# Fourteen matmuls on a cleared tile at the start, and the first norm's sums and spread half a unit later

## What is computed

```python
def hybrid_layer(h, pos, states, p):
    u = rms_norm(h, p['norm_mix']) @ p['w_in']
    ...                                  # four head groups on the columns of u
    h = h + concat([y_ssd, y_ret, y_gla, y_lru]) @ p['w_out']
    hn = rms_norm(h, p['norm_ffn'])
    return h + (silu(hn @ p['w_gate']) * (hn @ p['w_up'])) @ p['w_down']

def rms_norm(x, w):
    return x * rsqrt(mean(x * x) + EPS) * w
```

## Time and profile before

| | |
|---|---|
| median of 3 timed runs | 1326.43 us |
| range | 1326.39 to 1328.45 us |
| the profiled execution's own time | 1321.0 us |
| its span, first to last instruction | 1319.2 us |
| outside the span (1321.0 - 1319.2) | 1.8 us |
| PE busy | 1294.3 us, 98% of the span |
| DVE busy | 856.5 us, 65% |
| ACT busy | 706.6 us, 54% |
| POOL busy | 293.3 us, 22% |

### The profile page before, as it was taken

How to read it: one execution, slowest core, us unless ns; L and a number is a source line. 1 busy time by engine, 2 the same in 40 slices (tenths; PEclk the granted TensorE clock), 3 DMA queues, 4 the chain that set the end, 5 groups by cost and what they waited for, 6 DMA issues and landing times.

```text
span 1319.2 us, 26928 instructions
## 1 busy us (share of the span) xinstructions
PE 1294.3 (98%) x10781; PEld 1244.7 (94%) x10781; DVE 856.5 (65%) x1697; ACT 706.6 (54%) x1209; POOL 293.3 (22%) x248
## 2 busy tenths in 40 slices
PE   7999999999999999999999999999999999999996
PEld 7988898999999999999999888899999999999996
DVE  6745766478853885378757557655888358835864
ACT  7626355576642674266564264556766246624641
POOL 1101001112242224324411010001123412351250
PEclk9999989999999999999999999999999999999998
DMA  8855745557744774476567475447477347735741
GB/s 266 220 115 139 178 107 115 119 132 168 168 131 107 171 168 129 105 171 172 140 149 161 112 169 145 97 115 166 104 178 193 100 105 173 191 106 105 170 126 68
DMA packets 63387, 189.73 MB, mean 144 GB/s; under 512 B 7584, under 2 KB 8864, under 8 KB 63264
## 3 DMA queue, kind: packets, MB, share of 16 engines
q0 software_dynamic: 27936, 67.12, 30.9%
q1 hardware_dynamic: 30672, 111.95, 26.8%
q10 hardware_dynamic: 4656, 8.95, 2.3%
HBM read 180.33 MB, written 5.43 MB: 141 GB/s over the span
## 4 chain that ended last, share of the span: by engine, by line
PE 88%; DVE 5%; ACT 2%; DVEq 2%; DMA 1%; issue 1%; ACTq 0%
PE bank L1638 47%; PE bank L1667 32%; PE bank L1581 1%; DMA raw<-weights 1%; PE bank L1834 1%; DVE up L1511 1%; DMA wl<-weights 1%; PE bank L1955 0%; PE bank L1961 0%; PE bank L1599 0%; ACT wl L540 0%; PE bank L1593 0%; DVE h L1572 0%; DVE ct L989 0%; DVE lru_x L989 0%
## 5 line engine op out<-in xcount | busy, mean ns | idle before, releaser
L512 POOL DMA_DIRECT2D wl<-weights x194 | 168.2, 867 | 882.4 <-ACT wl L540 871.8
L1638 PE MATMUL bank<-xh,wh 128*128 128x272 f32 x800 | 242.9, 304 | 8.1 <-DVE xl L938 7.8
L541 ACT ACTIVATE wh<-raw 128x512 fp32r<-128x512 f32 (+1 forms) x243 | 197.8, 815 | 89.4 <-PE bank L1638 79.3
L1638 PE MATMUL bank<-xh,wl 128*128 128x272 f32 x800 | 234.1, 293 | 0.0
L1638 PE MATMUL bank<-xl,wh 128*128 128x272 f32 x800 | 233.6, 292 | 0.0
L540 ACT ACTIVATE wl<-raw 128x512 fp32r<-128x512 f32 (+1 forms) x192 | 145.8, 760 | 121.5 <-PE bank L1638 109.4
L1667 PE MATMUL bank<-xh,wl 128*128 128x272 f32 x704 | 203.1, 289 | 0.0
L1667 PE MATMUL bank<-xh,wh 128*128 128x272 f32 x704 | 202.8, 288 | 0.1
L1667 PE MATMUL bank<-xl,wh 128*128 128x272 f32 x704 | 202.8, 288 | 0.0
L1638 PEld LDWEIGHTS bank<-xh,wh 128*128 128x128 f32 x800 | 153.9, 192 | 19.4 <-issue 17.4
L541 ACT ACTIVATE wh<-wsum 128x512 fp32r<-128x512 f32 x176 | 105.2, 622 | 123.5 <-DVE wsum L1408 83.2
(11 more groups left out here) (404 smaller groups left out, 3015.1 us busy)
## 6 DMA issues: line engine op xcount, KB each, us to landing
raw<-weights SPq DMA_DIRECT2D x202, 512.0 KB, 6.1
wl<-weights POOLq DMA_DIRECT2D x132, 256.0 KB, 5.6
wl<-weights POOLq DMA_DIRECT2D x62, 512.0 KB, 7.4
h<-x SPq DMA_DIRECT2D x4, 544.0 KB, 6.1
y<-h SPq DMA_DIRECT2D x4, 544.0 KB, 2.7
rv<-rk ACTq DMA_DIRECT2D x8, 136.0 KB, 2.5
tz<-rq ACTq DMA_DIRECT2D x8, 136.0 KB, 5.4
S<-s_ssd ACTq DMA_DIRECT2D x2, 512.0 KB, 7.3
```

The costliest lines, as they stand in the source:

```text
L512: nc.gpsimd.dma_start(wl[:, place(j)], weights[n][:, lo:lo + width], accum_op=ALU.add).then_inc(lo_added[BLOCK0[j] % RING], 16)
L541: a(wh[:, place(j)], whole, ACT.Copy).then_inc(hi_done, 1)
L1638: ins = mm(bank_, wt[:, at:at + P], xx[:, cols], start=(i == 0 and pass_ == 0), stop=(i == len(ks) - 1 and pass_ == 2))
```

## The change

Four edits:

- `IDLE_MATMULS = 14` matmuls of 128x128 by 128x512 stand ahead of everything on TensorE. Their input is the last block of the `wl` ring, their output the bank M[1]. Nothing reads the result, and the next use of M[1] overwrites it.
- VectorE clears that block as its first instruction (a MEMSET of 128x512), and TensorE waits for it (`cleared`).
- The sums of the first norm move from after step 2 to after step 3, and the spread from after step 3 to after step 4.
- ScalarE's `hi_first(2)` moves from behind the eighth square to behind the fifth.

```diff
+IDLE_MATMULS = 14
...
+        x_rounded, exact_done, cleared = sem("x_rounded"), sem("exact_done"), sem("cleared")
+        idle_tile = wl[:, (RING - 1) * BLOCK:RING * BLOCK]
...
                 a(sq[:, m % 2, :] if m else sq_sum[:], h[:, m, :], ACT.Square).then_inc(h_squared.sem, 1)
-            hi_first(2)
+                if m == KT // 2:
+                    hi_first(2)
...
+            v.memset(idle_tile.bitcast(F32), 0.0).then_inc(cleared, 1)
             v.memset(sp_x[:], 0.0).then_inc(dense_free.sem, 3)
...
+            pe.wait_ge(cleared, 1)
+            for _ in range(IDLE_MATMULS):
+                mm(M[1][:], idle_tile[:, 0:P], idle_tile, start=True, stop=True)
+
...
-                    if (s, layer) == (2, 0):
+                    if (s, layer) == (3, 0):
                         square_sums(layer, -1)
                         last_squares(layer, -1)
-                    if (s, layer) == (3, 0):
+                    if (s, layer) == (4, 0):
                         pe.wait_ge(exact_done, 1)
                         spread_rstd(layer, -1)
```

More of the change, by code:

```diff
@@ L415, in trunk @@
             signal(n, 1) for n in ("cent_mm", "cent_first", "cent_second", "cent_out"))
-        x_rounded, exact_done = sem("x_rounded"), sem("exact_done")
+        x_rounded, exact_done, cleared = sem("x_rounded"), sem("exact_done"), sem("cleared")
+        idle_tile = wl[:, (RING - 1) * BLOCK:RING * BLOCK]
         y_final, y_stored = sem("y_final"), sem("y_stored")
```

## The result

The changed kernel took 1329.59 us (median of 16 runs, 1326.05 to 1331.5), the kernel before 1326.39 us in the same comparison (16 runs, 1319.05 to 1328.45). The ratio is 1.0030, 95% interval 1.0021 to 1.0039: slower, by more than the 0.2% that separates a change from none. In a later comparison the ratio was 1.0047 (1.0031 to 1.0064). Four executions in the experiments took 1788 to 4785 us; the ratios leave them out, the medians given include them and would be up to 0.6 us lower without.

The account below looks back on a forecast made before the run. Until 44 us the spread's time, through VectorE's and ScalarE's chain, was taken as the bound. Sums at 20.4 by TensorE, plus 1.0 for the lock, gave 21.4 against 19.63: +1.8 us on 1326.43, 1328.2 us; range 1326.4 to 1330.2.

Parts of the forecast that it names:

- The 14 matmuls raise the clock, and TensorE reaches unit 0 at 2.4 GHz: TensorE's start: 14 matmuls take 6.0 us, from 1.5 to 7.5, ahead of the first input; unit 0 then runs at 2.4 GHz.
- the end of the clear: VectorE's MEMSET ahead of the 14 matmuls: at most 0.7 us long, ending near 1.5 us, at no cost.
- the time of the sums by TensorE alone: End of unit 1: by TensorE alone the first norm's sums could start at 20.4 us, against 19.63 before.
- the reading that more is put ahead of the sums than is won: Units 0 and 1: 24 more matmuls (3.0 us) ahead of the sums outweigh the fast start, making sums 0.8 us later.
- The meeting of VectorE and GpSimd: Squares' additions: GpSimd's subtraction holds up VectorE, sixth addition ends at 21.3, sums start at 21.4; up to 1.0 us.
- The spread is 1.8 us late: First norm: spread follows the sums at a fixed distance, 26.7 in place of 24.91 us.
- a rival, at 0.22: Behind the sums: 3.2 us of near quiet makes TensorE's clock fall, +1.5 on 1.8, total +3.3 us, 1329.7; chance 0.22.
- the sign that I had named for being wrong: TensorE behind the sums: matmuls 0.23 us apart would show the forecast wrong.
- The size of the fall: Clock fall around the sums: 24 matmuls take 4.73 us in place of 3.2, priced at +1.5 us.
- This wait isn't the bound: Behind the spread: TensorE waits 2.4 us, is some 1.3 us late at 43.6, less than VectorE's 1.8.
- the two falls: Rival clock falls: behind the sums, total +3.3 us, chance 0.22; in the wait behind the spread, total +2.8 us, chance 0.08.
- The sum: Whole kernel: the spread's shift stays to the end, +1.8 us, 1328.2 us against the median; chance 0.43.

Follow-up runs that it names:

- with the wait filled: Kernel before plus the clear and 14 matmuls, with 7 unread 512-column matmuls in the wait ahead of the sums; 1324.92 us against 1324.53, ratio 1.0001.
- `hi_first(2)` last: Changed kernel with one edit undone: ScalarE's hi_first(2) behind the eighth square again; 1328.17 us against 1325.51 for the kernel before, ratio 1.0020.
- the moves alone: Changed kernel without the clear and the 14 matmuls; 1328.04 us, ratio 1.0019 to the kernel before.
- filled waits: Unread 512-column matmuls in TensorE's waits: changed kernel, both waits (ratio 1.0014) or the one ahead of the sums (1.0047); 14 matmuls without the moves (1.0001).

## Why the prediction was wrong, point by point

- **The 14 matmuls raise the clock, and TensorE reaches unit 0 at 2.4 GHz**: right, as was the end of the clear (1.40 us, at most 1.5 forecast), the time of the sums by TensorE alone (20.1, forecast 20.4) and the reading that more is put ahead of the sums than is won.
- **The meeting of VectorE and GpSimd**: right in place and size. The fifth addition took 2.42 us in the chain above, in place of 0.73, and ended 0.59 us behind GpSimd's operation (20.17 and 19.58); sums at 21.04, forecast 21.4.
- **"The spread is 1.8 us late"**: this step failed. It was 4.5 us late in the first trace (29.45 against 24.91). The step kept the 2.17 and the 3.11 us of the earlier trace rows from sums to spread. Measured were 3.08 and 5.33, at the low clock; in the other two traces 2.27 and 4.65, 2.48 and 5.60. I had the cause as a rival, at 0.22, with the right stretch, and took the more likely case to be that it doesn't come. It came in all three, and with it the sign that I had named for being wrong: matmuls 0.23 us apart behind the sums (24.51 and 24.74). What misled me was one trace: quiet of 2.2 us, no fall. I read it as a point from which to count; the second trace of the same kernel showed a fall with 0.67 us of waiting added.
- **The size of the fall**: also too small. I priced it at +1.5 us from 24 matmuls in 4.73 us. Here it lasted 3.4 or 6.8 us and also caught the sums; it cost 1.6 to 3.1 us up to the spread.
- **"This wait isn't the bound"**: failed with it. The wait behind the spread is 2.50 us as forecast (2.4), but the half behind it runs at the low clock, 4.6 to 4.7 us in place of 3.2, and TensorE becomes the bound of the start. I held the two falls to be alternatives; they come together.
- **The sum**: +1.8 us is about what the same order costs with the clock held up (+1.9 at the milestone for equal loads, in one trace). With the falls the milestone moves by 4.3. The time of 1329.59 lies in the range (1326.4 to 1330.2), but for another reason than the forecast's: I had given a change within 0.2% a chance of 0.62 and a loss beyond it 0.35. The trace that I worked from was of one of the fastest executions, 1321.0 us: by the estimate above its 6.8 us less of low clock behind the milestone are some 3.4 of the 10.2 us between the profiled spans, and no part of the change.

## What to carry to other kernels

Warming TensorE up ahead of its first input brought nothing that can be measured here (ratios 1.0005 and, with the wait filled, 1.0001). An engine that starts faster waits sooner, and here the wait, together with matmuls of one column, took the clock away again. Count the quiet on TensorE behind each thing that you speed up, one-column sums and small transposes included, though the page shows them as busy, and either fill the wait or leave the order in which it is covered. Don't let an addition of VectorE start while GpSimd's subtraction runs: here it took 2.42 us in place of 0.73. And where a kernel has several falls of the clock in an execution, read more than one trace before taking a stretch for undisturbed.

## What the runs showed of the hardware

- **Matmuls on zeros raise the clock.** 14 of them, 512 columns each, brought TensorE to 2.4 GHz in all eight usable traces that have them: the real matmuls behind them start 0.12 to 0.13 us apart from the second on. In the second trace of the changed kernel the 14 take 6.1 us, so there nearly all of them ran at the low level.
- **When it rises isn't fixed.** In three traces of the kernel before the first rise came after 26, 14 and 23 slow matmuls, at 13.6, 11.0 and 13.1 us. So the 2.6 us that a warm start could win are 1.4 in another execution (14 x 0.10).
- **What TensorE did before its clock fell.** Sums without a wait (2.2 us of one-column matmuls) never brought the clock down ahead of 40 us (first and third trace of before, the kernels with `hi_first(2)` last, with the moves alone and with filled waits). With a wait of 0.67 us or more ahead of them it fell in all six traces. Spread and 2.5 us of waiting (3.2 us) brought a fall in four of six, and what decided it the runs don't show. Why a fall lasts 3.4 us once and 6.8 us another time, the runs don't show.
- **The granted clock of the profile doesn't cover the start.** It is 1.00 over 7.77 to 13.60 us, where matmuls of 272 columns start 0.23 us apart.
